# Gelu values of an expert layer in two DRAM matrices, and one load for the two tiles of a group

## The reference

```python
s = jnp.einsum('thpd,hpnd->thpn', q, sub_keys)          # 8 heads, 2 x 128 keys
v1, i1 = lax.top_k(s[:, :, 0], 16); v2, i2 = lax.top_k(s[:, :, 1], 16)
vals, ci = lax.top_k(v1[..., :, None] + v2[..., None, :] ..., 16)
e = i1[ci // 16] * 128 + i2[ci % 16]                    # 16 of 16384 experts per head
g = jax.nn.softmax(vals, axis=-1)
act = jax.nn.gelu(jnp.einsum('td,thkd->thk', xc, u_tab[e])) * g
return jnp.einsum('thk,thkd->td', act, v_tab[e])
```

## Time and profile before

| | us |
|---|---|
| median of 3 runs | 3253.87 (3245.05 to 3258.52) |
| the profiled execution, its own time | 3263.77 |
| its span, first to last instruction | 3261.9 |
| PE busy | 3188.0 |
| DVE busy | 2016.6 |
| POOL busy | 1910.7 |
| ACT busy | 1240.0 |

### The profile page before, as it was taken

One profiled execution on the slowest core, in us unless ns is written; L12 is line 12 of the kernel. 1 busy time (PEld: TensorE's weight loads), 2 busy tenths in 40 slices (PEclk: granted clock), 3 DMA queues, 4 the chain that ended last, 5 costly groups with the idle time before them and its releaser, 6 DMA issues. The chain is left out here.

```text
span 3261.9 us, 47580 instructions
## 1 busy us (share of the span) xinstructions
PE 3188.0 (98%) x15034; PEld 2593.2 (79%) x15034; DVE 2016.6 (62%) x4049; ACT 1240.0 (38%) x1844; POOL 1910.7 (59%) x1318
## 2 busy tenths in 40 slices
PE   8889999999999999999899999999999999999999
PEld 7578888888888788888666778888888887887887
DVE  5567575752223888888646765767632225888888
ACT  3543333334344333333425743333332223333333
POOL 0005888888888656555000008888888886555554
PEclk9999999999999999999999999999999999999999
DMA  5915565566667999999418225656566668999998
GB/s 191 340 67 136 121 147 119 134 149 142 146 144 217 365 350 340 347 352 349 152 39 279 97 71 118 148 118 147 124 145 145 145 145 285 357 347 345 349 351 299
DMA packets 399382, 681.95 MB, mean 209 GB/s; under 512 B 145473, under 2 KB 239681, under 8 KB 399041
## 3 DMA queue, kind: packets, MB, share of 16 engines
q1 hardware_dynamic: 218944, 520.95, 46.7%
q0 software_dynamic: 155648, 134.82, 20.1%
q10 hardware_dynamic: 24704, 25.17, 2.3%
HBM read 560.85 MB, written 119.94 MB: 209 GB/s over the span
## 5 line engine op out<-in xcount | busy, mean ns | idle before, releaser
L1787 POOL DMA_INDIRECT gate_matrix<-pe_misc x768 | 1287.1, 1676 | 713.1 <-DVE pe_misc L2358 479.6
L2056 PE MATMUL psum<-split,ex_ah 128*128 128x512 f32 x2976 | 922.1, 391 | 14.0 <-DVE ex_al L2501 13.5
L431 PE MATMUL psum<-up_hhi,up_hi 128*128 128x512 f32 x2048 | 798.2, 390 | 0.0
L431 PE MATMUL psum<-up_hlo,up_hi 128*128 128x512 f32 x2048 | 796.9, 389 | 0.0
L431 PE MATMUL psum<-up_hhi,up_lo 128*128 128x512 f32 x2048 | 796.8, 389 | 0.0
L422 DVE TENSOR_TENSOR up_lo<-up_raw,up_hi 128x1024 fp32r<-128x1024 f32 x256 | 313.7, 1226 | 757.6 <-ACT up_hi L418 749.4
L2056 PEld LDWEIGHTS psum<-split,ex_ah 128*128 128x128 f32 x2976 | 555.1, 188 | 144.0 <-DVE ex_al L2501 29.3
L2056 PE MATMUL psum<-split,ex_al 128*128 128x512 f32 x1488 | 579.3, 389 | 0.0
L1797 POOL DMA_INDIRECT ex_gv<-in_v,ga_at x256 | 273.5, 1068 | 338.5 <-DVE x_sb L2451 320.1
L431 PEld LDWEIGHTS psum<-up_hhi,up_lo 128*128 128x128 f32 x2048 | 384.4, 188 | 79.7
L431 PEld LDWEIGHTS psum<-up_hhi,up_hi 128*128 128x128 f32 x2048 | 384.5, 188 | 79.4
(11 more groups left out here) (374 smaller groups left out, 3152.4 us busy)
## 6 DMA issues: line engine op xcount, KB each, us to landing
up_raw<-in_uT SPq DMA_DIRECT2D x256, 512.0 KB, 3.6
ro_wq<-in_v SPq DMA_DIRECT2D x256, 512.0 KB, 5.6
gelu<-up_z SPq DMA_DIRECT2D x256, 256.0 KB, 2.1
pe_misc<-gelu SPq DMA_DIRECT2D x256, 192.0 KB, 5.6
ex_gm<-gate_matrix SPq DMA_DIRECT2D x124, 384.0 KB, 5.9
gate_matrix<-ga_at ACTq DMA_DIRECT2D x8, 3072.0 KB, 13.4
gate_matrix<-ga_at SPq DMA_DIRECT2D x8, 3072.0 KB, 23.2
ro_wq<-in_peer_wq SPq DMA_DIRECT2D x32, 512.0 KB, 3.9
```

The costliest lines, as they stand in the source:

```text
L431: last = pe.matmul(self.ps[:, a, :], w[:, a, dc, :], h[:, dc, :], start=(dc == 0 and m == 0), stop=(dc == DC - 1 and m == 2))
L1787: pool.indirect_dma_start(place, bass.IndirectOffsetOnAxis(ap=to[:, j:j + 1], axis=0), gates[:, j:j + 1], None, compute_op=ALU.add).then_i ...
L2056: last = pe.matmul(psy[:, o, :], w[:, par, a, toks], v[:, par, a, cols], start=False, stop=(final and m == 2))
```

## The change

The matrix `gelu` becomes two: `gelu`, [128, 128 tiles, 384 dense tokens], and `gelu_last`, [128, 128 tiles, 128 last tokens]. In the first stage each gelu tile is stored by two DMAs, 1536 B and 512 B a partition, where one stored 2048 B; both count on the same semaphore, and every wait on it asks for twice as much. In the second stage one load brings the gelu values of both tiles of a group, 3072 B in one piece a partition, where two loads brought 1536 B a partition each. It is issued after the v load of the group's first tile and ahead of that of the second; DVE waits for it at the first tile alone. The gathers of single values read from `gelu_last`, with places worked out for it. The places of the other loads in SP's order stay.

```diff
--- before.py
+++ after.py
@@ UProducts
-        self.kept = [k.sig("up_kept0", 16), k.sig("up_kept1", 16)]
+        self.kept = [k.sig("up_kept0", 32), k.sig("up_kept1", 32)]
...
-        act.wait_ge(self.kept[a].sem, tile * 8 + (self.kept[a].base + 16 - 8 * a))
+        act.wait_ge(self.kept[a].sem, tile * 16 + (self.kept[a].base + 32 - 16 * a))
         act.activation(self.z[:, a, :], self.ps[:, a, :], ACT.Gelu_apprx_tanh).then_inc(self.gelued.sem, 1)
 
-    def keep(self, sp, zmat, tile, a):
+    def keep(self, sp, zmats, tile, a):
 
         sp.wait_ge(self.gelued.sem, tile + self.gelued.done(0))
-        sp.dma_start(zmat[:, bass.ds(tile, 1), :].rearrange("p a t -> p (a t)"), self.z[:, a, :]).then_inc(self.kept[a].sem, 16)
+        for zmat, toks in zip(zmats, (slice(0, SD), slice(SD, S))):
+            sp.dma_start(zmat[:, bass.ds(tile, 1), :].rearrange("p a t -> p (a t)"),
+                         self.z[:, a, toks]).then_inc(self.kept[a].sem, 16)
@@ peer
-    z_loaded = [[k.sig(f"ex_zload{p}{a}") for a in range(GT)] for p in range(2)]
+    z_loaded = [k.sig("ex_zload0"), k.sig("ex_zload1")]
...
-            def load_z(tile, par, a):
-                sp.dma_start(zz[:, par, a, :], zmat[:, bass.ds(tile, 1), 0:SD].rearrange("p a t -> p (a t)")
-                             ).then_inc(z_loaded[par][a].sem, 16)
+            def load_z(g, par):
+                sp.dma_start(zz[:, par, :, :], zmats[0][:, bass.ds(g * GT, GT), :]).then_inc(z_loaded[par].sem, 16)
...
             for a in range(GT):
                 load_v(a, a)
-            for t in range(2 * GT):
-                load_z(t, t // GT, t % GT)
+            for par in range(2):
+                load_z(par, par)
...
             for s in up.kept:
-                sp.wait_ge(s.sem, s.base + s.credit + 16 * NK // GT)
+                sp.wait_ge(s.sem, s.base + s.credit + 32 * NK // GT)
...
                     if g > 2:
                         sp.wait_ge(v_lo.sem, g * GT + v_lo.free(a))
                         load_v(g * GT + a, a)
-                    load_z(g * GT + a, g % 2, a)
+                    if a == 0:
+                        load_z(g, g % 2)
...
                     for a in range(GT):
                         sp.wait_ge(v_lo.sem, g * GT + v_lo.free(a))
                         load_v(g * GT + a, a)
-                        load_z(g * GT + a, par, a)
+                        if a == 0:
+                            load_z(g, par)
...
             for s in up.kept:
-                pool.wait_ge(s.sem, s.base + s.credit + 16 * NK // GT)
+                pool.wait_ge(s.sem, s.base + s.credit + 32 * NK // GT)
             for j in range(Z_AHEAD // 2):
-                ga.gather_z(pool, gz, zmat, j)
+                ga.gather_z(pool, gz, zmats[1], j)
...
-                    dve.tensor_scalar(ga.at_z[:, here], at[:, TD, :], float(S), token[:, TD:TT], ALU.mult, ALU.add)
+                    dve.tensor_scalar(ga.at_z[:, here], at[:, TD, :], float(P), token[:, 0:1], ALU.mult, ALU.add)
...
-                    dve.wait_ge(z_loaded[par][a].sem, z_loaded[par][a].base + 16)
+                    dve.wait_ge(z_loaded[par].sem, z_loaded[par].base + 16)
...
-                        dve.wait_ge(z_loaded[par][a].sem, i * 16 + z_loaded[par][a].base + 16)
+                        if a == 0:
+                            dve.wait_ge(z_loaded[par].sem, i * 16 + z_loaded[par].base + 16)
@@ build
-        zmat = nc.dram_tensor("gelu", (P, NK, S), F32, kind="Internal").ap()
+        zmats = [nc.dram_tensor(name, (P, NK, n), F32, kind="Internal").ap() for name, n in (("gelu", SD), ("gelu_last", P))]
```

More of the change, by code:

```diff
@@ L449, in finished @@
         for s in self.kept:
-            s.passed(16 * NK // GT)
+            s.passed(32 * NK // GT)
         for s in (self.hi_ready, self.lo_ready, self.dots, self.gelued):
@@ L1841, in reduced_angles, with peer @@
     return dve.tensor_scalar(out, out, pi, -pi, ALU.min, ALU.max)
-def peer(k, l, x, up, ga, misc, wq, wq_loaded, zmat, gmat, to, gates, rope, out):
+def peer(k, l, x, up, ga, misc, wq, wq_loaded, zmats, gmat, to, gates, rope, out):
     nc = k.nc
@@ L1926, in head @@
                     if not (first and j == 0):
-                        up.keep(sp, zmat, h * RT + (j - 1), (j - 1) % GT)
+                        up.keep(sp, zmats, h * RT + (j - 1), (j - 1) % GT)
                     if more and j == 1:
@@ L1956, in _ @@
                 up.load(sp, G0 + GT + j, j % GT)
-                up.keep(sp, zmat, G0 + j - 1, (j - 1) % GT)
+                up.keep(sp, zmats, G0 + j - 1, (j - 1) % GT)
             with sp.Fori(0, NP) as i:
@@ L1960, in _ @@
                     up.load(sp, i * GT + (G0 + ST + GT + a), a)
-                    up.keep(sp, zmat, i * GT + (G0 + ST + a - 1), (a - 1) % GT)
+                    up.keep(sp, zmats, i * GT + (G0 + ST + a - 1), (a - 1) % GT)
             for a in range(GT):
                 load_v(a, a)
-            for t in range(2 * GT):
-                load_z(t, t // GT, t % GT)
+            for par in range(2):
+                load_z(par, par)
             for done in ga.scattered[:TD - 1]:
@@ L1969, in _ @@
                 load_first_g(slice(0, SE), par, s_["early_gates"])
-            up.keep(sp, zmat, NK - GT - 1, (NK - GT - 1) % GT)
+            up.keep(sp, zmats, NK - GT - 1, (NK - GT - 1) % GT)
             for a in range(GT):
@@ L1973, in _ @@
                 load_v(GT + a, a)
-                up.keep(sp, zmat, NK - GT + a, a)
+                up.keep(sp, zmats, NK - GT + a, a)
             sp.wait_ge(ga.scattered[TD - 1].sem, ga.scattered[TD - 1].base + 16 * PH * TOPK)
@@ L2549, in peer @@
         s.passed(8 * NG)
-    for s in (z_loaded[0] + z_loaded[1]):
+    for s in z_loaded:
         s.passed(8 * NG)
@@ L2578, in early, with products @@
             self.up.first(sp, a)
-    def products(self, x, zmat, gmat, rope=None, out=None):
+    def products(self, x, zmats, gmat, rope=None, out=None):
         self.ga.open()
         to, gates = self.misc[:, 0, 0:PH * HW].bitcast(U32), self.misc[:, 1, 0:PH * HW]
-        peer(self.k, self.l, x, self.up, self.ga, self.misc, self.wq, self.wq_loaded, zmat, gmat, to, gates, rope, out)
+        peer(self.k, self.l, x, self.up, self.ga, self.misc, self.wq, self.wq_loaded, zmats, gmat, to, gates, rope, out)
         self.up.finished()
@@ L2617, in build @@
         if stop >= 2:
-            pe.products(x, zmat, gmat, rope)
+            pe.products(x, zmats, gmat, rope)
         if stop >= 3:
@@ L2635, in build @@
             if stop >= 4:
-                pe.products(x, zmat, gmat, out=out)
+                pe.products(x, zmats, gmat, out=out)
         if stop < 4:
```

## The result

| | us |
|---|---|
| before, median of 7 runs | 3256.18 (3245.05 to 3263.39) |
| changed, median of 7 runs | 3271.70 (3268.63 to 3276.89) |
| ratio | **1.0045**, 95% interval 1.0033 to 1.0056 |
| the profiled execution, its own time (span) | 3268.63 (3266.8) |

The change makes the kernel **slower by 0.45%**, some 15 us, where I had forecast 6 us less; the measured time lies above the range. It is just short of the 0.5% that I had called the limit of a measurement, but seven runs a side keep the whole interval above 1.

A forecast was written before the change was run, and what follows sets the result against it. PE bounds the kernel, losing time only in the v products to the loop round a v buffer. Packets gave -6.4 us, all other terms 0: from the 3253.9 us median to 3247.5 us, range 3236 to 3268.

The forecast's parts named there:

- step 1: v products: fewer gelu packets spare 65 ns a group, shortening awaited v landings; -6.4 us, bounds 0 and -15.3.
- step 2: SP's load order in the v products: second v up to 0.51 us later, next first v as much earlier; 0.
- step 5: Joint of the stages: gates issued earlier, but the queued v and gelu bytes stay; 0, -1 to +1 in each layer.
- The bound: v products: PE's group of 8.16 us nearly equals the v buffer's loop; PE can regain 15.3 us at most.
- Rival B: v products: nothing is given back, PE's losses come from something packets do not change; 3253.9 us, chance 0.22.
- Rival C: v products: slower, second tile's v lands later behind the pair and the first does not make it up; 3279 us, chance 0.10.
- My evenness argument: SP's queue: 896 KB between successive v loads each way, where it was 704 and 1088; taken as 0.
- Step (3): v products: first tile's gelu values land 0.51 us later, within 1.8 us spare before DVE uses them; 0.
- Step (4): u products: two stores a tile, some 0.55 us more on SP 256 times, hidden by the u matmuls; 0.
- Rival D: v products: PE's whole loss goes, -15.3 and a us in each joint; 3236.6 us, chance 0.13.

The follow-up runs named there:

- gates by tile: Split-store kernel with POOL's second-layer v gathers waiting for the first gates; gates loaded one tile at a time behind their own v: 0.9974 to before, 3249.4 us.
- split stores, order alone: Two matrices and stores, single gelu loads; both tiles' loads moved behind the group's first v: 1.0034 to before, against 1.0004 with each behind its own v.
- both with the gathers held back: Changed kernel, and split stores with single gelu loads, each with POOL's first second-layer v gathers waiting for the first gates: 1.0024 and 0.9997 to before.
- paired load alone: Kernel before, one matrix and one store, with one gelu load for both tiles between the two v loads: 1.0036 to before, 3269.6 us.
- the pair ahead of the first v: Changed kernel with the paired gelu load right behind the gates and ahead of the group's first v load: 1.0073 to before, 3285.8 us.
- the gates behind the first v: Split-store kernel with POOL's second-layer gathers waiting for gates; the group's whole gates load moved behind its first v load: 1.0002 to before, 3259.6 us.
- the swapped waits: Two matrices and stores, single gelu loads, with ACT's wait for the stores put ahead of its wait for the products: 1.0014 to before, 3261.6 us.
- the split stores alone: Two matrices and two stores as in the changed kernel, but one gelu load a tile behind its v as before: 1.0004 to before, 3261.7 us.

## Why the prediction was wrong

The change was forecast 6.4 us faster and measured 15 us slower. Three terms of the sum failed: packets at -6.4 us (step 1), the order of the loads at 0 (step 2) and the joint at 0 (step 5).

**The bound was right.** PE's own pace in the u products, a v loop nearly as long as PE's group, some 15 us to be had at most: gates by tile took 8 us of them with 3958 of 3970 matmuls.

**Step (1), fewer packets, -6.4 us, failed.** The price of a packet came from stretches at the start with less in the queues. ACT's queue was not even alone there: SP's had 18.5% beside its 55.4% from 30 to 160 us, and the second slice of the earlier trace rows reads 9, so the v products are not the only place at nine tenths, as I had written. In the steady loop the same bytes in 13% fewer packets took the same share of the engines, 97.2%: the 7.2 ns that I took for a packet's fixed cost are in the medians (2 x 65 against 121 ns), but on the mean 3072 B cost 140.8 ns in one packet and 132.2 in two. Of the 65 ns a group nothing was spared, and so nothing of the forecast's gain came. Rival B had this right: the engines were not short of time as such, and gates by tile runs at 358 GB/s with more packets, 454167 in the whole kernel against 417814 in the changed one. That also answers the Trainium skill's 358 GB/s as a limit per core ("DMA: Bandwidth & Descriptors", "Specifications"): the same rate is reached here with the loss nearly gone, so no run shows it binding in the changed kernel at 347, and the kernel before lies above it, at 383 GB/s, from 1055 to 1100 us.

**Step (2), the order, 0 us, is the step that failed most.** By the medians it is worth 9 to 12 us: 0.30% (split stores, order alone), 0.27% (both with the gathers held back), 0.36% (paired load alone). I argued that the work ahead of v(a=0) falls as that ahead of v(a=1) rises, a sum that does not change. Rival C had the place of the load and the sign at 0.10, priced at 32 us: too much. (With its own numbers the sign turns at 6.4 / 124 = 0.05 us a group; the 0.13 that I gave is the 0.5% of a measurement.) Its mechanism is not what the traces show. Its sign was a landing above 6 us at the second tile; the landings there take 5.68 us on the mean from 1100 to 1400 us, 5.62 before, and ACT waits longer at the first tile, 1.22 and 1.15 us for 1.02 and 1.09, and no longer at the second.

**What the runs show in place of step (2)** is that the place alone costs, 0.30% between two runs that differ in nothing else; by what path the early 192 KB lengthen the wait at the first tile is not shown. My evenness argument was half right: with 896 KB to each tile the loop does run best, but only where each load follows its own v; the paired load evened the sums by asking for 192 KB some 4 us before it had to.

v's landing is a poor witness: its median was 5.7 us before and after. PE's matmuls in a window tell more. ACT's wait for v (180.0 and 175.4 us before, 188.3 and 189.1 after, 156.3 with gates by tile) goes with them in these three, but not everywhere: the slowest run, with the pair ahead of the first v, has 187.4, and the gates behind the first v have 163.8 for no gain.

**Step (3)** held: no wait for gelu values in the steady loop of the changed kernel. The paired load alone, with its 1536 B packets, has eight, 5.1 us in all. **Step (4)** held for PE, 500 of 500 us, but it was not without effect: I costed the second store's DMA and issue and overlooked the register for the wait's value, which moves the scatters, shown for the second layer alone. **Step (5), the joint, 0 within 1 us, failed:** it took the gates' landing to depend on the queue of v and gelu loads ahead of it, whose bytes stay. The second of them takes 13.8 us for 6.5, and the joint is 5 us longer. POOL's eight gathers stood 2 us behind the gates' issue before and 9 us ahead of it after. The earlier trace rows show POOL waiting only 7.4 us for the last store; it is 21.3 after. By the ratios the early gathers are worth 2 to 7 us of it. **Rival D** was wrong for this change; the better order gives half of its 17 us.

What stays open: why moving all the gates behind the first v gained nothing, when small gates behind each v gained 0.26%. Two things speak to it, neither tested. DVE's product waits 5.8 us for gelu there, which can be a part at most. And by the sums of step (2) that run has 1088 KB behind the first v and 704 behind the second, the uneven split of the kernel before turned round. Open as well: why the swapped waits do not give the whole joint back and leave the first layer's scatters early, and why the split stores alone run the steady loop faster.

## What to carry to other kernels

Where the DMA queue is nearly full and each turn of a loop waits for one load, try the order of the loads before the number of packets: put each load just behind the most urgent one of its own tile, and do not merge loads if that brings bytes forward. Judge by the medians of some ten executions, and by the work done in fixed windows over two or more, not by the landing time, which stood at 5.7 us here. Where two engines fill the queue in a race, as at the joint here, a wait that fixes the winner is worth a try: it gave some 7 us in the changed kernel.

## What the runs showed that I had not expected

A scatter on POOL takes 1547 ns, and up to 2588 in the second layer, where it falls together with work on DVE. One from the head shown above, before the change (POOL, then DVE):

```profile
2051.11 2.36 POOL L1787 DMA_INDIRECT gate_matrix<-pe_misc  x1 [0.30 <-issue]
```

```profile
2050.82 1.23 DVE L422 TENSOR_TENSOR up_lo<-up_raw,up_hi 128x1024 fp32r<-128x1024 f32 x1
```

After it, DVE's L422 starts 0.3 us behind the scatter instead of 0.3 ahead of it, and the scatter takes 1.55. In the second layer 67 of the 384 scatters took over 1600 ns before the change and 56 after it, and the last one ends 11 us earlier, in both profiles of each kernel. A gelu that comes 1.3 us later once a head, by nothing but a register between two waits, goes with it. And packets of 3072 B did not save the fixed cost that the prices of 1019 B and 3919 B packets at the start had given.
